# Delta rule of a hybrid encoder on Trainium2: the triangular inverse by 64x64 products accumulated in PSUM, and the loop over heads written out

## The reference

```python
m = jnp.where(strict, jnp.einsum('bhncd,bhnsd->bhncs', k_beta, k) * decay, 0.0)
t_inv = lax.linalg.triangular_solve(eye + m, eye, left_side=True, lower=True, unit_diagonal=True)
u = t_inv @ v_beta
w = t_inv @ (k_beta * jnp.exp(g)[..., None])
...
def step(state, inp):
    v_new = u_c - w_c @ state
    o = q_dec @ state + attn_intra @ v_new
    state = state * g_last + k_dec.T @ v_new
```

## Time and profile before

| | us |
|---|---|
| runs of the kernel before, median of 3 | 1642.01 (1640.67 to 1643.83) |
| span of the profiled execution | 1642.3 |
| PE busy in it | 1578.3 (96%) |
| DVE, ACT, POOL busy | 623.9, 585.8, 577.7 |
| one head of the delta stage in the loop | 52.58 |
| seven such heads | 368 |

### The profile page before, as it was taken

The page is one execution under the profiler, slowest core; times in us unless marked ns, Lnnn a source line. Parts: engine busy times, 40 slices in busy tenths (PEclk is TensorE's granted clock), DMA queues, the critical chain, the costliest instruction groups (busy, mean ns, idle before and its releaser), DMA issues.

```text
span 1642.3 us, 21292 instructions
## 1 busy us (share of the span) xinstructions
PE 1578.3 (96%) x7900; PEld 1293.9 (79%) x7900; DVE 623.9 (38%) x1014; ACT 585.8 (36%) x956; POOL 577.7 (35%) x286
## 2 busy tenths in 40 slices
PE   6899999999998989999999999999989999999998
PEld 6868878887787668888888887777668888888887
DVE  3336555655555432222022224677532222112210
ACT  5542343233332433323223234554533322222321
POOL 4522322223220233544444444211124444544432
PEclk9999999999999999999999999999999999999999
DMA  6421101111010123332432234111113332333222
GB/s 241 125 69 39 52 26 38 38 51 51 25 34 1 39 69 104 103 103 71 122 103 90 76 91 125 46 39 30 30 46 103 101 103 79 114 103 101 81 79 87
DMA packets 39209, 124.26 MB, mean 76 GB/s; under 512 B 4192, under 2 KB 5472, under 8 KB 39136
## 3 DMA queue, kind: packets, MB, share of 16 engines
q1 hardware_dynamic: 38976, 123.00, 24.7%
q10 hardware_dynamic: 160, 0.26, 0.1%
HBM read 120.89 MB, written 2.10 MB: 75 GB/s over the span
## 4 chain that ended last, share of the span: by engine, by line
PE 85%; DVE 6%; ACT 5%; issue 2%; POOL 0%; DMA 0%; DVEq 0%; SPq 0%; ACTq 0%
PE bank L548 66%; ACT ws L1046 4%; PE bank L713 3%; PE bank L711 2%; PE bank L699 2%; DVE ws L1434 2%; PE bank L979 1%; PE bank L847 1%; DVE ws L1437 1%; DVE act_lo L1434 1%; PE bank L810 1%; DVE ws L1428 1%; DVE ws L1431 1%; PE bank L736 1%; PE bank L560 1%
## 5 line engine op out<-in xcount | busy, mean ns | idle before, releaser
L480 POOL TENSOR_TENSOR w_lo<-w_raw,w_hi 128x1024 fp32r<-128x1024 f32 (+1 forms) x250 | 537.8, 2168 | 953.3 <-ACT w_hi L1046 953.0
L548 PE MATMUL bank<-act_hi,w_hi 128*128 128x512 f32 (+1 forms) x1776 | 705.8, 397 | 9.9 <-POOL w_lo L480 4.4
L548 PE MATMUL bank<-act_hi,w_lo 128*128 128x512 f32 (+1 forms) x1776 | 682.0, 384 | 0.0
L548 PE MATMUL bank<-act_lo,w_hi 128*128 128x512 f32 (+1 forms) x1776 | 681.7, 384 | 0.0
L548 PEld LDWEIGHTS bank<-act_hi,w_hi 128*128 128x128 f32 x1776 | 337.3, 190 | 77.0 <-issue 7.6
L548 PEld LDWEIGHTS bank<-act_hi,w_lo 128*128 128x128 f32 x1776 | 336.7, 190 | 66.0
L548 PEld LDWEIGHTS bank<-act_lo,w_hi 128*128 128x128 f32 x1776 | 337.5, 190 | 64.0 <-issue 5.1
L1046 ACT ACTIVATE w_hi<-w_raw 128x1024 fp32r<-128x1024 f32 (+1 forms) x250 | 230.4, 953 | 89.0 <-PE bank L548 86.6
L1428 DVE TENSOR_TENSOR ws<-bank,ws 128x512 f32<-128x512 f32 x126 | 86.9, 690 | 371.5 <-PE bank L548 320.8
L1046 ACT ACTIVATE ws<-ws 128x512 f32<-128x512 f32 (+3 forms) x143 | 94.3, 670 | 189.9 <-DVE ws L1428 121.9
L1675 DVE TENSOR_TENSOR xT<-xT,bank 128x512 f32<-128x512 f32 (+1 forms) x48 | 33.0, 688 | 271.6 <-PE bank L548 271.6
(11 more groups left out here) (145 smaller groups left out, 1250.2 us busy)
## 6 DMA issues: line engine op xcount, KB each, us to landing
w_raw<-w_stream SPq DMA_DIRECT2D x154, 512.0 KB, 3.6
w_raw<-w_out SPq DMA_DIRECT2D x32, 384.0 KB, 3.2
w_raw<-w_down SPq DMA_DIRECT2D x32, 384.0 KB, 3.1
w_raw<-w_down SPq DMA_DIRECT2D x32, 320.0 KB, 3.2
ws<-x_in SPq DMA_DIRECT2D x1, 2048.0 KB, 8.6
ws<-mem_in SPq DMA_DIRECT2D x2, 512.0 KB, 4.4
out<-ws SPq DMA_DIRECT2D x1, 1024.0 KB, 4.2
sq_c<-squares_in SPq DMA_DIRECT2D x1, 768.0 KB, 6.9
```

What stands on the lines that cost most here:

```text
L480: nc.gpsimd.tensor_tensor(w_lo[:, s, 0:width * P], w_raw[:, s, 0:width * P], w_hi[:, s, 0:width * P].bitcast(F32), ALU.subtract).then_inc( ...
L548: mm = nc.tensor.matmul(acc, wt[:, c % RING, wsl], at[:, act0(k0 + k), off:off + n], start=(start and k == 0 and m == 0), stop=(stop and k ...
```

## The change

The inverse is done on 64x64 pieces. `r` = 0 is the upper left corner of each 128x128 tile (partitions and columns 0 to 63), `r` = 1 the lower right one. Both are inverted by levels 1 to 5. Since the masks of these levels are zero outside the two corners, nothing is lost. The last level fills the lower left corner from the two, in two products.

- `T` and `Z` stay in PSUM: `diagonal(0)` writes ZZ and its transpose to banks `D[4]` (r = 0) and `D[5]` (r = 1), and `diagonal(k)` adds the correction to them (`start` is false). The level masks therefore carry the factor -1.
- After each level the accumulators are copied out: the corners r = 0 by ACT, r = 1 by DVE. Before, DVE subtracted from SBUF. The mask is applied per corner by DVE.
- Since `D[4]` and `D[5]` are now held through the inverse, the three products that empty them (`VB`, `KBG`, `KDEC`) come earlier on DVE.
- The fill is dealt out anew, by the tables `AFTER_P` and `AFTER_TZ`.
- The first seven heads are written out on all engines (`each_head`) in the place of `turns`.

```diff
-            turns(pe, DN_HEADS - 1, lambda h: delta(h, lambda j, ks: proj_dn(h + 1, j, ks)))
+            each_head(lambda h: delta(h, lambda j, ks: proj_dn(h + 1, j, ks)))
...
+                def diagonal(level):
+
+                    for t in range(NT):
+                        for r in range(2):
+                            t_acc = bank[half_rows(r), D[4 + r], HB * t:HB * (t + 1)]
+                            z_acc = bank[half_rows(r), D[4 + r], SEQ // 2 + HB * t:SEQ // 2 + HB * (t + 1)]
...
+                                if level < LEVELS - 2 or r == 0:
+                                    block_matmul(t_acc, half_tile(ZZ, t, r), half_tile(PM, t, r), False)
+                                mm = block_matmul(z_acc, half_tile(PM, t, r), half_tile(ZZ, t, r), False)
...
-                transposes4(D[2], ZZ).then_inc(S.t_tr, 1)
-                fill(1, range(6, 8))
+                fill(1, range(4, 6))
+                for k in range(1, LEVELS - 1):
...
+                    for t in range(NT):
+                        for r in range(2):
+                            mm = block_matmul(bank[half_rows(r), D[2 + r], HB * t:HB * (t + 1)],
+                                              half_tile(MM, t, r), half_tile(TT, t, r), True)
...
+                    for j, ks in AFTER_P[k - 1]:
+                        fill(j, ks)
+                    pe.wait_ge(S.p_done, 2 * n + 2)
+                    diagonal(k)
+                    for j, ks in AFTER_TZ[k - 1]:
+                        fill(j, ks)
...
-                    fill(3, range(t + 1, t + 2))
+                    if t == 0:
+                        fill(3, range(7, 8))
...
-                fill(3, range(5, 8))
...
+                for k in range(1, LEVELS - 1):
+                    act.wait_ge(S.tz_mm, 10 * h + 2 * k - 1)
+                    a(tz_of(0), tz_bank(0), ACT.Copy).then_inc(S.tz_upper, 1)
+                    if k == 3:
+                        fill(2)
...
+                    for r in range(2):
+                        dve.wait_ge(S.p_mm, n + r + 1)
+                        mul(half(PM, r), p_bank(D[2 + r], r),
...
+                    if k < LEVELS - 2:
+                        cp(tz_of(1), tz_bank(1)).then_inc(S.tz_lower, 1)
```

More of the change, by code:

```diff
@@ L325, in turns, with each_head @@
                 body(n - 1)
+        def each_head(body):
+            for h in range(DN_HEADS - 1):
+                body(h)
         def w(i):
@@ L528, in _ @@
             rows_of(0)
-            turns(pool, DN_HEADS - 1, lambda h: delta(h, True))
+            each_head(lambda h: delta(h, True))
             delta(DN_HEADS - 1, False)
@@ L687, in delta @@
                 pe.wait_ge(S.z_done, h + 1)
+                pe.wait_ge(S.vb_done, h + 1)
+                pe.wait_ge(S.kbg_done, h + 1)
+                pe.wait_ge(S.kdec_done, h + 1)
+                diagonal(0)
                 pe.wait_ge(S.dm_pre, 2 * h + 1)
-                transposes4(D[2], ZZ).then_inc(S.t_tr, 1)
-                fill(1, range(6, 8))
[L691 to L717, removed]
@@ new lines, in delta @@
+                pe.wait_ge(S.tz_upper, 5 * h + 5)
+                pe.wait_ge(S.tz_lower, 5 * h + 5)
+                for t in range(NT):
+                    mm = block_matmul(bank[half_rows(1), D[2], HB * t:HB * (t + 1)], half_tile(MM, t, 0, 1),
+                                      half_tile(TT, t, 0), True)
+                mm.then_inc(S.p6_mm, 1)
+                fill(3, range(5, 6))
+                pe.wait_ge(S.p6_done, h + 1)
+                for t in range(NT):
+                    mm = block_matmul(bank[half_rows(0), D[3], HB * t:HB * (t + 1)], half_tile(PM, t, 1, 0),
+                                      half_tile(ZZ, t, 1), True)
@@ L722, in delta @@
+                mm.then_inc(S.z6_mm, 1)
+                fill(3, range(6, 7))
+                pe.wait_ge(S.z6_done, h + 1)
                 for t in range(NT):
@@ L1222, in _ @@
             squares_qk(0)
-            turns(act, DN_HEADS - 1, lambda h: delta(h, lambda j: conv_tile(h + 1, j), True))
+            each_head(lambda h: delta(h, lambda j: conv_tile(h + 1, j), True))
             def mem_square(layer, j):
@@ L1551, in delta @@
                 mul(w4(VB), psum4(D[4]), dn_bcast(BETA, h)).then_inc(S.vb_done, 1)
+                dve.wait_ge(S.ktr_done, h + 1)
+                mul(w4(KBG), psum4(D[5]), dn_bcast(NBEG, h)).then_inc(S.kbg_done, 1)
+                mul(w4(KDEC), psum4(D[5]), dn_bcast(EDEC, h)).then_inc(S.kdec_done, 1)
                 dve.wait_ge(S.dm_done, h + 1)
@@ new lines, in delta @@
+                for k in range(1, LEVELS - 1):
+                    n = 10 * h + 2 * (k - 1)
+                    for r in range(2):
+                        dve.wait_ge(S.p_mm, n + r + 1)
+                        mul(half(PM, r), p_bank(D[2 + r], r),
+                            sq_c[half_rows(r), LEVEL0 + k:LEVEL0 + k + 1, HB * r:HB * (r + 1)].to_broadcast([HB, NT, HB])
+                            ).then_inc(S.p_done, 1)
+                    if 2 <= k <= 4:
+                        fill(1, k - 1)
+                    if k == 5:
+                        fill(2, 1)
+                    dve.wait_ge(S.tz_mm, n + 2)
+                    if k < LEVELS - 2:
+                        cp(tz_of(1), tz_bank(1)).then_inc(S.tz_lower, 1)
+                    else:
+                        cp(half(ZZ, 1), tz_bank(1)[:, 1]).then_inc(S.tz_lower, 1)
```

96 lines of the change are left out of this document (58 added, 38 removed).

## The result

| | before | after |
|---|---|---|
| median of the runs, us | 1641.34 (1640.20 to 1643.83, 4 runs) | 1654.48 (1654.18 to 1657.98, 4 runs) |
| ratio of the times | | 1.0086, 95% interval 1.0072 to 1.0100 |
| span of the profiled execution | 1642.3 | 1656.2 |
| head 6, from sum matmul to sum matmul | 52.58 | 52.96 |
| the last head, sum to sum | 45.09 | 54.80 |

The changed kernel is slower, by 13.1 us of the medians. The forecast was slower by 47. The profiled execution after is the slowest of its four, 3.5 us above their median. Its span is 13.9 us longer than before: 0.8 up to the first sum matmul (173.04 before, 173.82 after), 1.7 over the six heads between the first sum and the seventh (316.10 and 317.77), 9.7 in the last head, and 1.7 in all that comes behind it (1108.1 and 1109.8).

The account below looks back on a forecast made before the run. PE's order was taken to bound seven loop heads, the PE-DVE chain the eighth. 7 x (3.4 + 2.1) + 8.3 = +47 us on 1642 gave 1689 us; range 1616 to 1714 (own range 1661 to 1714).

Parts of the forecast that it names:

- What does one record take: PE's 64x64 products in the inverse: 0.0625 us per record, 280 records a head, 17.5 us.
- rival 1: Opposite corners of the inverse run at once: 0.031 us per record, 8.75 instead of 17.5, total 1619 us; chance 0.18.
- Rival 2: Half overlap: PE starts in order, only neighbouring records of two corners overlap; 11.0 us of records, total 1637 us; chance 0.14.
- Shape changes: PE changes tile shape 26 times a head around 13 groups of small products, 0.08 each: 2.1 us, bounds 0 and 2.6.
- rival 4: Dearer 64x64 records, 0.073 us each as by L979: +3.1 for each of eight heads, total 1714 us; chance 0.15.
- Waits: PE's exposed waits for copies and masks in a loop head's inverse: 1.1 us instead of 1.7.
- Conv taps fit beside the updates: DVE's convolution taps (0.74) were to fit beside the inverse's update products.
- Stretch two: From the product with the keys (L723) to the sum matmul, one fill step left of seven: 8.2 against 6.1, +2.1 us a head.
- Sum of a head: Each of seven loop heads: +3.4 us up to the product with the keys and +2.1 from there to the sum matmul.
- Stretch one: From the inverse's transposes to the product with the keys (L723), without fill: 20.7 instead of 17.3, +3.4 us a head.
- Last head: The eighth head's inverse, without fill, as a chain: 30.4 instead of 22.14, +8.3 us; lower clock could cost some more.
- Loops written out: Writing out the first seven heads instead of looping: 0, bounds 1.0 us a head won or no loss.

Follow-up runs that it names:

- last_head_fill: The changed kernel with eight steps of the second memory projection moved from behind the delta stage into levels 1 to 3 of the last head; 1652.42 us (1.0065).

## Why the prediction was wrong

- **"What does one record take", 0.0625.** This is the step that failed. It is 0.031, which is rival 1 (chance 0.18). I took the row of four tiny transposes (0.063 from one to the next) for what the instructions cost. It was no floor: two records of different corners start less than 0.01 us apart, and a pair takes 0.058. (The four transposes all lie in the same 16 rows.) By the groups measured above, 280 records take 1.0 + 5 x 0.5 + 4 x 1.0 + 0.96 + 1.06 = 9.5 us, not 17.5. The bound by columns (0.056) was the right price of one corner (0.0585). Rival 2's ground, that PE starts in order and so only neighbours overlap, failed too: in the second phase four records of one corner stand before four of the other, and the cadence is the same 0.032. In the group at 458.98 the record that carries the upper corner's semaphore is the 28th in the program and the 31st to start.
- **Shape changes, 2.1.** 3.9. I took from the earlier trace rows the distance up to the first record behind the change, but the record itself takes 0.10 longer. The trace before shows it in the same place: the first record of L979 has 0.27 to the next start, the others 0.163. The 0.177 of the forecast is the mean of these; 0.163 is 1.5 times the 0.109 of the 128 columns of L1005, so the dearer record of rival 4 had no ground.
- **Waits, 1.1, and "Conv taps fit beside the updates".** The copies and masks fit nearly everywhere: in head 6 three groups start 0.05 later than the shape change explains and one 0.11, some 0.3 in all. The taps do on DVE, but I didn't ask whose bank the last one frees: 1.74 us in each of seven heads.
- **Stretch two, +2.1.** Right: 8.74 with one step, against 8.2 + 0.7, so +1.9.
- **Sum of a head, +5.5.** +0.38 in head 6, +0.28 in the mean of six. Stretch one is 9.5 of records, 3.9 of shape changes and 2.0 of waits, 15.4; measured, it is 28.8 (454.07 to 482.85) less 19 steps of 0.70, 15.5. Against the 17.3 of before that is -1.8. With stretch two the sum is +0.1, and some 0.2 lie in the rest of the head.
- **Last head, +8.3.** +9.7, for another reason. I took 0.0625 at a high clock and put the clock down as "some more"; the records are 0.055 there ((2.03 - 0.31) / 31) because the clock is at its lower level. With the clock at 0.96, the same head is 2.5 above before. That the number came close is luck.
- **Loops written out, 0.** Right for the old body, the only one that was tried both ways.

The sign came out right by luck, since the mechanism was rival 1's, which gave 1619. The inverse did get cheaper in seven heads, and waits, moved fill and the last head's clock took back more than it gave.

## What to carry to other kernels

After a cut in the bounding engine's work, ask for each PSUM bank who frees it and at which level, and move the freeing work with the table. Put the spread work where one step hides most: in this scan, whose turns wait for two engines, three steps cost a quarter of their length; behind a group that waits for nothing a step costs all of it. And look at the granted clock of a stretch that has become a chain of short products: there work that is due anyway can pay for itself. In `last_head_fill` eight steps (5.6 us) went into the last head and it became 3.0 us shorter.

## What the runs showed of the hardware

- Two 64x64 fp32 products in opposite corners of the array run side by side: a pair of records every 0.058 us, 0.031 a record with the first interval, and 0.058 a record where one corner works alone (0.066 with the first interval). The mean length that the profile's page gives for such a record, 235 ns, says nothing of that.
- A group of 64x64 products between 128x512 records costs 0.30 us beside its own records: 0.10 ahead of it, 0.11 behind it, and 0.10 more up to the second record behind it.
- PE busy for 19.03 of 29.90 us with small products had its clock at 0.54, and the whole last head stood at 0.69; with 12 products of 128x384 between the small ones it stood at 0.96. In the loop the clock fell in one head each of three profiled executions, behind a wait of 1.3 to 1.7 us.
- Copies out of PSUM on 64 partitions cost as much as on 128. DVE's copies by shape (busy us, mean ns):

```profile
L1516 DVE COPY ws<-bank 64x512 f32<-64x512 f32 x32 | 22.2, 694 | 57.1 <-PE bank L731 57.1
L1516 DVE COPY ws<-bank 128x512 f32<-128x512 f32 x29 | 20.0, 689 | 21.8 <-PE bank L912 9.5 <-PE bank L797 7.1 <-PE bank L593 5.0
```
